# One part of a value table as dense tiles and a scattered weight matrix, the rest gathered, in a hybrid decoder layer

## The chip, the cores and the metric

The kernel runs on one core of a Trainium2 chip. The metric is the device time of one execution in microseconds (us), as a median of several runs; less is better.

## The reference, cut to what matters

The layer ends with a product-key (PEER) expert network over 256 tokens of width 2048, in two chunks c of 128 tokens. Each of 8 heads gives a token 16 experts out of 128 x 128 = 16384; an expert's number is 128 times its first key plus its second key, both from 0 to 127.

```
u = jnp.take(expert_u, ic, axis=0)                 # (c, k, d): 128 tokens x 128 experts x 2048
act = jax.nn.gelu(jnp.einsum('ckd,cd->ck', u, xc), approximate=False)
vv = jnp.take(expert_v, ic, axis=0)
return jnp.einsum('ck,ckd->cd', gc * act, vv)
```

A row of either table is 8 KB. What is added to the layer's state h is, for each token, the sum over its 128 experts of a weight (gate times activation) times the expert's value row. A final norm follows.

## The kernel before, in words

Everything ahead of the expert network (mixer, attention, cross-attention, the query projection `peer_wq`) is the same in both kernels. Work is ordered by hand: each engine has its own program, and they meet at semaphores.

The expert network is cut into GROUPS = 16 groups, one for each chunk c (2) and head (8). A group has TOP = 16 experts for each of the 128 tokens, which lie on the 128 partitions. For one k of a group, one indirect DMA gathers 128 rows of the table, one to each partition: 1 MB. So there are 256 gathers from the key table `peer_u` (u) and 256 from the value table `peer_v` (v). Both are issued by GpSimd (POOL).

- `u_ring` and `v_ring` have 4 slots of 1 MB each. In `period(p, q)` POOL issues, for k = 0 to 15 in turn, `gather_u` of group p (which waits until VectorE has done with the slot's last row, `dot_done`) and `gather_v` of group p - 1 (which waits for TensorE, `v_used`). POOL's program is in order: a gather behind one that waits has to wait as well.
- VectorE (DVE), in its own `period`, waits for the last values of the group before (`v_landed`), copies the indices for v, forms the weights (`weights`), finds the experts of the next group (`route`, a chain of some 30 short instructions) and their gates (`gates`), and then does 16 `dot_products` (L1079), one for each landed u slot.
- ScalarE (ACT) makes for each v gather a diagonal matrix of that k's weights (`diagonals`, L634); TensorE (PE) multiplies it with the v slot in four matmuls of 512 columns (L1493) and sums over all k in four PSUM banks, `misc` for chunk 0 and `acc` for chunk 1.
- In the last group 8 of the 16 value gathers (`BY_DVE`) are added by VectorE with a multiply-add over 2048 columns (L1167), the others by TensorE (L1501), so that both work on what lands last. `finish(0)` (the final norm of chunk 0) runs on VectorE between groups 13 and 15, `finish(1)` at the end.
- Loops over pairs of groups are hardware loops (`Fori`).

Of the kernel before, what the change touches and what calls it, by code (L numbers as in the profile page):

```python
# [33 lines left out]
def hybrid_layer(  # L34
# [8 lines left out]
    P = 128  # L43
# [13 lines left out]
    TOP = 16  # L57
# [84 lines left out]
    v_ring = put("v_ring", [P, 4, D], F32, at_split)  # L142
    final_gain = put("final_gain", [P, D], F32, at_raw)
# [23 lines left out]
    pT = put("pT", [P, 2, 3 * P], F32)  # L167
    xmax = put("xmax", [P, 2, TT], F32)
# [14 lines left out]
    picked = put("picked", [P, 2, TOP], F32)  # L183
# [6 lines left out]
    idx_u = put("idx_u", [P, 2, TOP], U32)  # L190
    idx_v = put("idx_v", [P, 2, TOP], U32)
    dots = put("dots", [P, 2, TOP], F32)
    acts = put("acts", [P, 2, TOP], F32)
    wts = put("wts", [P, 2, TOP], F32)
# [7 lines left out]
    with ExitStack() as ctx:  # L202
# [28 lines left out]
        v_landed = [sem(f"v_landed{s}") for s in range(4)]  # L231
        routed, idx_v_ready, nbest_ready, gexp_done = sem("routed"), sem("idx_v_ready"), sem("nbest_ready"), sem("gexp_done")
# [37 lines left out]
        BY_DVE = [2, 5, 8, 11, 12, 13, 14, 15]  # L270
        BY_PE = [k for k in range(TOP) if k not in BY_DVE]

        PC = CH * ITEMS["peer"][1]
        AHEAD = 12

# [7 lines left out]
        def _(sp):  # L286
# [71 lines left out]
        def _(pool):  # L358
# [23 lines left out]
            nc.gpsimd.memset(fones[:, :], 1.0).then_inc(consts, 1)  # L382
            nc.gpsimd.iota(iota[:, :], pattern=[[1, TOP]], base=0, channel_multiplier=0,
# [13 lines left out]
            def gather_u(p, q, k, fresh=False):  # L397
                if not (fresh and k < 4):

                    wait_apart(pool, dot_done, p * TOP + (k - 3))  # L400
                nc.gpsimd.indirect_dma_start(  # L401
                    out=u_ring[:, k % 4, :], out_offset=None, in_=u_rows,
                    in_offset=bass.IndirectOffsetOnAxis(ap=idx_u[:, q, k:k + 1], axis=0)).then_inc(u_landed[k % 4], 16)

            def gather_v(g, q, k, fresh=False):
                if not (fresh and k < 4):
# [6 lines left out]
            def period(p, q):  # L413
                pool.wait_ge(routed, p + 1)
                pool.wait_ge(idx_v_ready, p)
                for k in range(TOP):
                    gather_u(p, q, k)
                    gather_v(p - 1, 1 - q, k)

# [4 lines left out]
            for k in range(TOP):  # L424
                gather_u(0, 0, k, fresh=True)
            pool.wait_ge(routed, 2)
            for k in range(AHEAD):
                gather_u(1, 1, k)

            pool.wait_ge(idx_v_ready, 1)  # L430
            pool.wait_ge(peer_used, PC)
            for k in range(TOP):
                gather_v(0, 0, k, fresh=True)
                if k + AHEAD < TOP:
                    gather_u(1, 1, k + AHEAD)
            with pool.Fori(1, GROUPS // 2) as b:
                period(b * 2, 0)
                period(b * 2 + 1, 1)
            pool.wait_ge(idx_v_ready, GROUPS)
            for k in range(TOP):  # L440

                if k - 4 in BY_DVE:
# [1089 lines left out]
```

## Time and profile before

| what | value |
|---|---|
| median of 3 runs | 2108.12 us (2105.76 to 2112.22) |
| the profiled execution, its own time | 2111.71 us |
| span of its profile | 2109.9 us |
| its mean granted TensorE clock | 0.97 |
| TensorE, VectorE, ScalarE, GpSimd busy | 84%, 50%, 23%, 43% of the span |

The expert network takes the second part of the span, from about 750 us on. Shares of busy time are means over stages with different limits, so the stages are read one by one.

### The profile page before, as it was taken

To read this page: it belongs to the slowest core of one execution; us is meant where nothing else is said; L and a number is where in the kernel's file an instruction comes from. 1 tells how busy PE (TensorE), PEld (TensorE's weight loads), DVE (VectorE), ACT (ScalarE), POOL (GpSimd) and SP (SyncE) were. 2 spreads that over 40 slices of the span, in tenths; PEclk is the share of its full clock that TensorE was granted. 3 is DMA by queue.
4 is the path that set the end of the run, shared out by engine and by line. 5 is a ranking of instruction groups with operands and counts; after the bars stand their busy time and mean duration, and the time that the engine had idled before them with its cause. 6 is when DMAs were issued, how large, how long until landed. Compare 5 with 4: busy or idle time off the path is not lost.

```text
span 2109.9 us, 20817 instructions
## 1 busy us (share of the span) xinstructions
PE 1776.5 (84%) x7158; PEld 1134.4 (54%) x7161; DVE 1057.3 (50%) x1504; ACT 487.1 (23%) x802; POOL 911.5 (43%) x642
## 2 busy tenths in 40 slices
PE   7999999999999999797777777777777777758774
PEld 7998799888998898432332232322323223323232
DVE  4438343233333257534664664664664654655444
ACT  5345253345434411110110110111111111120111
POOL 4444143444432324444545545534535535535332
PEclk9999799999999999999999999999999999999998
DMA  8996154555535689999999999999999999999997
GB/s 204 235 194 158 67 182 160 195 187 189 167 120 194 195 331 391 364 368 422 414 415 423 416 422 421 420 420 421 416 419 421 417 422 415 420 421 382 422 414 274
DMA packets 150703, 682.56 MB, mean 324 GB/s; under 512 B 14632, under 2 KB 19824, under 8 KB 84336
## 3 DMA queue, kind: packets, MB, share of 16 engines
q0 software_dynamic: 73728, 536.90, 62.0%
q1 hardware_dynamic: 76912, 144.82, 23.1%
q8 instruction: 39, 0.64, 0.1%
q14 instruction: 24, 0.20, 0.0%
HBM read 679.58 MB, written 2.10 MB: 323 GB/s over the span
## 4 chain that ended last, share of the span: by engine, by line
PE 50%; DMA 34%; DVE 6%; issue 6%; POOL 2%; ACT 0%; DVEq 0%; SPq 0%; POOLq 0%; ACTq 0%
DMA v_ring<-in_peer_v_dram,idx_v 29%; PE acc L1493 6%; PE misc L1493 5%; PE acc L1202 5%; PE acc L1204 5%; PE acc L1203 5%; PE acc L1210 5%; PE acc L1209 5%; PE acc L1211 5%; PE acc L1471 4%; DMA u_ring<-in_peer_u_dram,idx_u 4%; PE acc L1432 1%; POOL u_ring L401 1%; DVE product L1079 1%; DMA raw<-in_w_in_dram 1%
## 5 line engine op out<-in xcount | busy, mean ns | idle before, releaser
L1079 DVE CUSTOM_DVE_ANT_0 product<-u_ring,hn 128x2048 bf16<-128x2048 f32 x256 | 586.7, 2292 | 497.3 <-DMA u_ring<-in_peer_u_dram,idx_u 491.4
L1493 PE MATMUL misc<-v_ring,diag 128*128 128x512 f32 x1024 | 480.3, 618 | 146.1 <-DMA v_ring<-in_peer_v_dram,idx_v 112.9
L1493 PE MATMUL acc<-v_ring,diag 128*128 128x512 f32 x896 | 423.9, 621 | 142.3 <-DMA v_ring<-in_peer_v_dram,idx_v 106.8
L409 POOL DMA_INDIRECT v_ring<-in_peer_v_dram,idx_v x240 | 283.6, 1182 | 436.4 <-PE misc L1493 216.6
L367 POOL TENSOR_TENSOR w_lo<-raw,w_hi 128x1024 fp32r<-128x1024 f32 x112 | 273.7, 2445 | 443.3 <-ACT w_hi L461 442.9
L401 POOL DMA_INDIRECT u_ring<-in_peer_u_dram,idx_u x256 | 325.7, 1272 | 263.7 <-DVE dots L1079 132.1
L1493 PEld LDWEIGHTS misc<-v_ring,diag 128*128 128x128 f32 x1024 | 192.2, 196 | 433.8 <-issue 259.4
L1493 PEld LDWEIGHTS acc<-v_ring,diag 128*128 128x128 f32 x896 | 168.7, 196 | 397.3 <-issue 230.8
L461 ACT ACTIVATE w_hi<-raw 128x1024 fp32r<-128x1024 f32 x224 | 236.8, 1059 | 337.6 <-PE acc L1211 151.3
L723 DVE TENSOR_TENSOR w_lo<-raw,w_hi 128x1024 fp32r<-128x1024 f32 x112 | 153.6, 1371 | 298.5 <-ACT w_hi L461 298.4
L634 ACT ACTIVATE diag<-ident,wts 128x128 f32<-128x128 f32 x240 | 91.4, 398 | 749.9 <-PE misc L1493 391.2
L1202 PE MATMUL acc<-t_hi,w_hi 128*128 128x256 f32 x896 | 255.7, 285 | 0.2 <-issue 0.2
L1203 PE MATMUL acc<-t_lo,w_hi 128*128 128x256 f32 x896 | 253.9, 283 | 0.0
L1204 PE MATMUL acc<-t_hi,w_lo 128*128 128x256 f32 x896 | 253.8, 283 | 0.0
L1209 PE MATMUL acc<-w_hi,t_hi 128*128 128x512 f32 x448 | 175.3, 391 | 0.0
L1211 PE MATMUL acc<-w_hi,t_lo 128*128 128x512 f32 x448 | 174.5, 389 | 0.0
L1210 PE MATMUL acc<-w_lo,t_hi 128*128 128x512 f32 x448 | 174.4, 389 | 0.0
L1202 PEld LDWEIGHTS acc<-t_hi,w_hi 128*128 128x128 f32 x896 | 172.3, 192 | 0.7 <-issue 0.4
L1203 PEld LDWEIGHTS acc<-t_lo,w_hi 128*128 128x128 f32 x896 | 172.3, 192 | 0.1
L1204 PEld LDWEIGHTS acc<-t_hi,w_lo 128*128 128x128 f32 x896 | 172.2, 192 | 0.0
L1211 PEld LDWEIGHTS acc<-w_hi,t_lo 128*128 128x128 f32 x448 | 84.1, 188 | 17.5
L1209 PEld LDWEIGHTS acc<-w_hi,t_hi 128*128 128x128 f32 x448 | 84.2, 188 | 17.3
(223 smaller groups left out, 1117.1 us busy)
## 6 DMA issues: line engine op xcount, KB each, us to landing
raw<-in_w_in_dram SPq DMA_DIRECT2D x64, 512.0 KB, 6.7
raw<-in_xattn_wk_dram SPq DMA_DIRECT2D x32, 512.0 KB, 4.2
raw<-in_xattn_wv_dram SPq DMA_DIRECT2D x32, 512.0 KB, 3.7
raw<-in_w_out_dram SPq DMA_DIRECT2D x32, 512.0 KB, 4.3
raw<-in_xattn_wq_dram SPq DMA_DIRECT2D x32, 512.0 KB, 4.2
raw<-in_xattn_wo_dram SPq DMA_DIRECT2D x32, 512.0 KB, 4.2
praw<-in_peer_wq_dram SPq DMA_DIRECT2D x32, 512.0 KB, 8.7
u_ring<-in_peer_u_dram,idx_u POOLq DMA_INDIRECT x256, 16.3
```

Of the source, the lines that this page charges most:

```text
L367: nc.gpsimd.tensor_tensor(w_lo[:, j % RING, :, :], raw[:, j % RING, :, :], w_hi[:, j % RING, :, :].bitcast(F32), ALU.subtract).then_inc(lo ...
L401: nc.gpsimd.indirect_dma_start(out=u_ring[:, k % 4, :], out_offset=None, in_=u_rows, in_offset=bass.IndirectOffsetOnAxis(ap=idx_u[:, q, k: ...
L409: nc.gpsimd.indirect_dma_start(out=v_ring[:, k % 4, :], out_offset=None, in_=v_rows, in_offset=bass.IndirectOffsetOnAxis(ap=idx_v[:, q, k: ...
L461: nc.scalar.activation(w_hi[:, j % RING, :, :], raw[:, j % RING, :, :], ACT.Copy).then_inc(hi_done, 1)
L1079: nc.vector.tensor_tensor_reduce(out=product[:, :], in0=u_ring[:, k % 4, :], in1=hn[:, c, :], scale=1.0, scalar=0.0, op0=ALU.mult, op1=ALU ...
L1202: nc.tensor.matmul(o, wh, hi[:, kt, :], start=first and ct % 2 == 0, stop=False, skip_group_check=True)
L1203: nc.tensor.matmul(o, wh, lo[:, kt, :], start=False, stop=False, skip_group_check=True)
L1204: ins = nc.tensor.matmul(o, wl, hi[:, kt, :], start=False, stop=last and ct % 2 == 1, skip_group_check=True)
L1209: nc.tensor.matmul(o, xh, w_hi[:, s, kk, :], start=first, stop=False)
L1210: nc.tensor.matmul(o, xh, w_lo[:, s, kk, :], start=False, stop=False)
L1211: ins = nc.tensor.matmul(o, xl, w_hi[:, s, kk, :], start=False, stop=last)
L1493: ins = nc.tensor.matmul(o, diag[:, k % 4, :], v_ring[:, k % 4, n * CW:(n + 1) * CW], start=False, stop=False)
```

## The change

Of the 128 first keys the last DENSE = 40 (88 to 127, FROM = 88) are no longer gathered. Their 40 x 128 value rows are loaded once, in order, as 40 tiles of 128 rows (1 MB each, `tile_landed`, from the SP queue, into the four slots of `u_ring` once the dot products are over). Each tile is multiplied by a 128 x 128 matrix of weights that has, for every second key and token, the token's weight of that expert: `wT0` and `wT1`, one for each chunk, [key, 40 tiles, token].

- These matrices are made in batches of WB = 8 tokens (32 batches in all). The lists of first keys, second keys and weights are transposed by TensorE (`turn_lists`) and copied by VectorE (`take_lists`); VectorE compares them with a row of key numbers (`one_hots`: one compare of 1024 columns, one compare and one multiply of 320 columns), TensorE multiplies the two one-hot matrices (`scatter_weights`, 8 matmuls of 40 columns) and ScalarE copies the result (`weights_T`). The 16 batches of chunk 0 stand between the dot products of groups 8 to 15, those of chunk 1 behind the last dot product.
- All 256 value gathers are still issued, but with a bound: `bounds_check` names the last row of first key 87, and `oob_is_err=False`. Their weight is set to zero where the first key is 88 or more (`low_wts`), so that whatever the slot holds there counts for nothing.
- Chunk 0's 128 value gathers go to TensorE through four slots, 8 in each of periods 2 to 7 and 10 in each of periods 8 to 15 (`v_share`), in POOL's order between the u gathers of that period. Before, each period had 16.
- Chunk 1's 128 value gathers are all issued behind the last dot product, into six slots (`V2S`), and VectorE adds them one by one with a multiply-add over 2048 columns (`add_values`); eight of them stand between the 16 last batches of `one_hots`. In that time TensorE multiplies the 40 tiles, each for both chunks (8 matmuls of 512 columns; for the last four tiles chunk 1's come after chunk 0's).
- `finish(0)` and `finish(1)` both stand at the end of VectorE's program, and the hardware loops are written out.

The core of the diff:

```
-            def gather_v(g, q, k, fresh=False):
-                if not (fresh and k < 4):
-                    wait_apart(pool, v_used, g * TOP + (k - 3))
+            def gather_v(n, slot, landed):
                 nc.gpsimd.indirect_dma_start(
-                    out=v_ring[:, k % 4, :], out_offset=None, in_=v_rows,
-                    in_offset=bass.IndirectOffsetOnAxis(ap=idx_v[:, q, k:k + 1], axis=0)).then_inc(v_landed[k % 4], 16)
+                    out=v_slot(slot), out_offset=None, in_=v_rows,
+                    in_offset=bass.IndirectOffsetOnAxis(ap=idx[:, n // TOP, n % TOP:n % TOP + 1], axis=0),
+                    bounds_check=FROM * KEYS - 1, oob_is_err=False).then_inc(landed, 16)
...
+            for p in range(1, GROUPS):
+                pool.wait_ge(routed, p + 1)
+                share = v_share(p)
+                for k in range(TOP):
+                    gather_u(p, k)
+                    for n in share[k * len(share) // TOP:(k + 1) * len(share) // TOP]:
+                        if n >= VS:
+                            pool.wait_ge(v_used, n - VS + 1)
+                        elif n == 2:
+                            pool.wait_ge(peer_used, PC - CH)
+                        gather_v(n, n % VS, v_landed[n % VS])
+            for m in range(TILE0):
+                if m >= V2S:
+                    pool.wait_ge(v_added, m - V2S + 1)
+                elif m < VS:
+                    pool.wait_ge(v_used, TILE0 - VS + m + 1)
...
+                gather_v(TILE0 + m, m % V2S, late_landed[m % V2S])
...
+            for t in range(DENSE):
+                if t < 4:
+                    sp.wait_ge(dot_done, GROUPS * TOP - 4 + t + 1)
+                else:
+                    sp.wait_ge(tile_used, t - 3)
+                sp.dma_start(u_ring[:, t % 4, :], v_rows[(FROM + t) * KEYS:(FROM + t + 1) * KEYS, :]).then_inc(tile_landed[t % 4], 16)
...
+            def period(g):
+                q, c = g % 2, g // PH
+                weights(g - 1)
+                if g + 1 < GROUPS:
...
+                    route(g + 1, 1 - q, (g + 1) // PH, (g + 1) % PH)
+                    gates(g + 1, 1 - q)
+                if g < PH:
+                    dot_products(g, q, c, range(0, TOP))
+                else:
+                    dot_products(g, q, c, range(0, 6))
+                    if g == PH:
+                        take_lists(0)
+                    one_hots(2 * (g - PH))
+                    dot_products(g, q, c, range(6, 12))
+                    one_hots(2 * (g - PH) + 1)
+                    dot_products(g, q, c, range(12, TOP))
...
+            def add_values(m):
+                dve.wait_ge(late_landed[m % V2S], 16 * (m // V2S + 1))
+                if m:
+                    dve.wait_ge(v_added, m)
+                nc.vector.scalar_tensor_tensor(y_sum[:, 1, :], v_slot(m % V2S), low_wts[:, PH + m // TOP, m % TOP:m % TOP + 1],
+                                               (y_sum if m else h)[:, 1, :], ALU.mult, ALU.add).then_inc(v_added, 1)
...
+            weights(GROUPS - 1)
+            take_lists(1)
+            for b in range(BATCHES):
+                one_hots(BATCHES + b)
+                if b % 2:
+                    add_values(b // 2)
+            for m in range(BATCHES // 2, TILE0):
+                add_values(m)
+            dve.wait_ge(v_added, TILE0)
             finish(0)
...
+            def one_hots(b):
+                t, q = b % BATCHES * WB, b % 2
+                if b >= 2:
+                    dve.wait_ge(wT_done, b - 1)
+                nc.vector.tensor_tensor(hotA[:, q, :, :], listsT[:, 1, t:t + WB].unsqueeze(2).to_broadcast([P, WB, KEYS]),
+                                        keys[:, :].unsqueeze(1).to_broadcast([P, WB, KEYS]), ALU.is_equal)
+                step(nc.vector.tensor_tensor(hotB[:, q, :, :], listsT[:, 0, t:t + WB].unsqueeze(2).to_broadcast([P, WB, DENSE]),
+                                             keys[:, FROM:].unsqueeze(1).to_broadcast([P, WB, DENSE]), ALU.is_equal))
+                nc.vector.tensor_tensor(hotB[:, q, :, :], hotB[:, q, :, :], listsT[:, 2, t:t + WB].unsqueeze(2).to_broadcast([P, WB, DENSE]),
+                                        ALU.mult).then_inc(hot_ready, 1)
...
+            def scatter_weights(b):
+                pe.wait_ge(hot_ready, b + 1)
...
+                for t in range(WB):
+                    ins = nc.tensor.matmul(acc[:, 0, b % 2, t * DENSE:(t + 1) * DENSE], hotA[:, b % 2, t, :], hotB[:, b % 2, t, :],
+                                           start=True, stop=True)
...
+            def dense_tile(t, c):
+                for i, o in enumerate((low, high)[c]):
+                    ins = nc.tensor.matmul(o, wT[c][:, t, :], u_ring[:, t % 4, i * CW:(i + 1) * CW], start=c == 1 and t == 0, stop=t == DENSE - 1)
...
+            for b in range(BATCHES, 2 * BATCHES):
+                scatter_weights(b)
+            pe.wait_ge(wT_copied, 2 * BATCHES)
+            for t in range(DENSE):
+                pe.wait_ge(tile_landed[t % 4], 16 * (t // 4 + 1))
+                ins = dense_tile(t, 0)
+                if t < DENSE - 4:
+                    dense_tile(t, 1).then_inc(tile_used, 1)
```

## Rows read from the trace of the kernel before

**Rows 1.** The page's table of slices: DMA share and GB/s, 52.7 us each.

```profile
DMA  8996154555535689999999999999999999999997
GB/s 204 235 194 158 67 182 160 195 187 189 167 120 194 195 331 391 364 368 422 414 415 423 416 422 421 420 420 421 416 419 421 417 422 415 420 421 382 422 414 274
```

**Rows 2.** Windows: us, busy time and count by engine, clock, DMA share, GB/s.

```profile
922.40:1962.90 1040.50, 784.46 (x1666) 312.65 (x1666) 594.15 (x899) 124.03 (x282) 511.02 (x416) 0.96 1.01 417
1482.40:1493.90 11.50, 7.78 (x19) 3.26 (x21) 9.03 (x40) 3.16 (x8) 2.73 (x3) 0.91 1.01 420
...
900.00:920.00 20.00, 20.00 (x48) 8.92 (x47) 0.00 (x0) 4.88 (x8) 6.58 (x7) 1.00 0.90 306
1520.00:1560.00 40.00, 29.84 (x66) 11.55 (x65) 18.40 (x16) 3.69 (x7) 16.70 (x17) 1.00 1.01 422
```

**Rows 3.** Groups by line, 780 to 2110 us: busy us, mean ns, idle before.

```profile
L1079 DVE CUSTOM_DVE_ANT_0 product<-u_ring,hn 128x2048 bf16<-128x2048 f32 x252 | 577.6, 2292 | 487.3 <-DMA u_ring<-in_peer_u_dram,idx_u 481.5 <-DVE gate L1060 2.7 <-DVE dots L1079 0.3
...
L401 POOL DMA_INDIRECT u_ring<-in_peer_u_dram,idx_u x248 | 317.9, 1282 | 218.8 <-DVE dots L1079 120.0 <-issue 72.5 <-PE misc L1493 17.1
...
L1167 DVE SCALAR_TENSOR_TENSOR y_sum<-v_ring,wts,y_sum 128x2048 f32<-128x2048 f32 x6 | 14.1, 2351 | 22.6 <-DMA v_ring<-in_peer_v_dram,idx_v 22.5
...
L1051 DVE TENSOR_TENSOR hot<-hot,top_at 128x512 f32<-128x512 f32 x15 | 10.4, 692 | 0.5
...
L1113 DVE TENSOR_TENSOR y_out<-y_sum,final_gain 128x1024 f32<-128x1024 f32 x2 | 2.5, 1226 | 0.2
```

**Rows 4.** VectorE's timeline, one period's seam (1478 to 1500 us).

```profile
1480.14 2.29 DVE L1079 CUSTOM_DVE_ANT_0 product<-u_ring,hn 128x2048 bf16<-128x2048 f32 x1 [2.67 <-DMA u_ring<-in_peer_u_dram,idx_u]
1482.36 0.08 DVE L1079 DVE_READ_ACCUMULATOR2_ANT dots<- 128x1 f32 x1
1482.69 0.17 DVE L1087 COPY idx_v<-idx_u 128x16 uint32<-128x16 uint32 x1 [0.25 <-DMA v_ring<-in_peer_v_dram,idx_v]
...
1493.85 2.29 DVE L1079 CUSTOM_DVE_ANT_0 product<-u_ring,hn 128x2048 bf16<-128x2048 f32 x1 [0.26 <-DVE gate L1060]
...
1496.19 2.29 DVE L1079 CUSTOM_DVE_ANT_0 product<-u_ring,hn 128x2048 bf16<-128x2048 f32 x1
```

**Rows 5.** GpSimd's timeline over the same seam.

```profile
1483.55 0.94 POOL L401 DMA_INDIRECT u_ring<-in_peer_u_dram,idx_u  x1 [0.30 <-issue]
1487.09 0.94 POOL L409 DMA_INDIRECT v_ring<-in_peer_v_dram,idx_v  x1 [2.60 <-PE misc L1493]
1496.96 2.33 POOL L401 DMA_INDIRECT u_ring<-in_peer_u_dram,idx_u  x1 [8.93 <-PE acc L1493]
```

**Rows 6.** The u gathers of 920 to 2045 us: issue to landing.

```profile
DMA to landing us min/median/max: 7.1/16.3/18.7
```

**Rows 7.** The last value gathers, 2050 to 2110 us: issue to landing.

```profile
DMA to landing us min/median/max: 5.5/8.2/9.9
```

**Rows 8.** The page's DMA queues: packets, MB, share of 16 engines.

```profile
q0 software_dynamic: 73728, 536.90, 62.0%
```

**Rows 9.** VectorE's timeline around the start of group 2.

```profile
859.65 2.29 DVE L1079 CUSTOM_DVE_ANT_0 product<-u_ring,hn 128x2048 bf16<-128x2048 f32 x1 [0.23 <-DMA u_ring<-in_peer_u_dram,idx_u]
...
872.07 2.29 DVE L1079 CUSTOM_DVE_ANT_0 product<-u_ring,hn 128x2048 bf16<-128x2048 f32 x1
...
884.52 2.29 DVE L1079 CUSTOM_DVE_ANT_0 product<-u_ring,hn 128x2048 bf16<-128x2048 f32 x1 [2.66 <-DMA u_ring<-in_peer_u_dram,idx_u]
```

**Rows 10.** TensorE's timeline, 900 to 920 us: values only.

```profile
899.66 20.76 PE L1493 MATMUL misc<-v_ring,diag 128*128 128x512 f32 x48
```

**Rows 11.** The chain that ended last, its last pieces: start, us, what.

```profile
2099.48 2.75 DVE y_sum L1108 x4
2102.28 0.04 issue
2102.32 1.24 DVE y_out L1113
...
2104.40 1.28 DVE y_out L1120
```

**Rows 12.** VectorE's timeline: the last dot product.

```profile
2048.02 2.29 DVE L1079 CUSTOM_DVE_ANT_0 product<-u_ring,hn 128x2048 bf16<-128x2048 f32 x1 [2.65 <-DMA u_ring<-in_peer_u_dram,idx_u]
```

More of the change, by code:

```diff
@@ L382, in _ @@
             nc.gpsimd.memset(fones[:, :], 1.0).then_inc(consts, 1)
+            nc.gpsimd.iota(keys[:, :], pattern=[[1, KEYS]], base=0, channel_multiplier=0,
+                           allow_small_or_imprecise_dtypes=True)
             nc.gpsimd.iota(iota[:, :], pattern=[[1, TOP]], base=0, channel_multiplier=0,
@@ L639, in gelu, with period @@
                 nc.scalar.activation(acts[:, q, :], dots[:, q, :], ACT.Gelu, scale=rstd[:, c:c + 1]).then_inc(gelu_done, 1)
-            def period(p, q, c, second=False, last=False):
-                if second:
-                    diagonals(p - 1, 1 - q, range(4), fresh=True)
-                if not last:
+            def period(p):
+                if p + 1 < GROUPS:
                     gate_exp(p + 1)
-                diagonals(p - 1, 1 - q, range(4 if second else 0, TOP))
-                gelu(p, q, c)
+                share = v_share(p)
+                diagonals(share[:4])
+                if p >= PH:
+                    weights_T(2 * (p - PH))
+                    diagonals(share[4:7])
+                    weights_T(2 * (p - PH) + 1)
+                    diagonals(share[7:])
+                else:
+                    diagonals(share[4:])
+                gelu(p, p % 2, p // PH)
             def finish(c):
@@ new lines, in _, with take_values, turn_lists @@
+            low = [misc[:, n, :] for n in range(4)]
+            high = [acc[:, n // 2, n % 2, :] for n in range(4)]
+            def take_values(n):
+                pe.wait_ge(v_landed[n % VS], 16 * (n // VS + 1))
+                pe.wait_ge(diag_ready, n + 1)
+                for i, o in enumerate(low):
+                    ins = nc.tensor.matmul(o, diag[:, n % 4, :], v_slot(n % VS)[:, i * CW:(i + 1) * CW], start=False, stop=False)
+                ins.then_inc(v_used, 1)
+            def turn_lists(c):
+                pe.wait_ge(wts_ready, (c + 1) * PH)
+                for a in range(3):
+                    ins = nc.tensor.transpose(acc[:, 1, 0, a * P:(a + 1) * P], lists[:, a, c, :], ident[:, :])
+                ins.then_inc(lists_done, 1)
@@ new lines, in _ @@
+            for o in low:
+                nc.tensor.matmul(o, zeros[:, 0:P], zeros[:, :], start=True, stop=False)
+            for p in range(2, GROUPS):
+                share = v_share(p)
+                if p == PH:
+                    turn_lists(0)
+                for n in share[:4]:
+                    take_values(n)
+                if p >= PH:
+                    scatter_weights(2 * (p - PH))
+                    for n in share[4:7]:
+                        take_values(n)
+                    scatter_weights(2 * (p - PH) + 1)
+                    for n in share[7:]:
+                        take_values(n)
+                else:
+                    for n in share[4:]:
+                        take_values(n)
@@ new lines, in _ @@
+            turn_lists(1)
+            for b in range(BATCHES, 2 * BATCHES):
+                scatter_weights(b)
[5 more added lines that the diff above has]
+                    dense_tile(t, 1).then_inc(tile_used, 1)
+            ins.then_inc(y_done, 1)
+            for t in range(DENSE - 4, DENSE):
+                ins = dense_tile(t, 1)
```

221 lines of the change are left out of this document (80 added, 141 removed).

## Prediction

> **What bounds the kernel now.** I read the page's slices first: in the expert network the DMA engines are full and move 414 to 423 GB/s in almost every slice [rows 1]. Windows confirm it for 13 whole periods: 1040.5 us at DMA share 1.01, while TensorE is busy for 75% and VectorE for 57% of it [rows 2]. The groups by line say who pays: VectorE is idle for 481.5 us in front of its dot products, waiting for u rows [rows 3]. So this stage moves bytes. One gather of 1.049 MB costs 1.049/0.422 = 2.48 us of the full DMA [rows 2]; a period of 32 gathers costs 80 us (1040.5/13). Fewer bytes should mean less time, as long as the engines stay full. Whether they do is the second question, and the timelines answer it. At a period's seam VectorE does no dot product from 1482.4 to 1493.85 us, 11.4 us of weights, routing and gates [rows 4]; no u slot comes free, and POOL issues nothing between 1488.0 and 1496.96 us [rows 5]. The DMA nevertheless stays at 1.01 [rows 2], because up to 8 MB are asked for at that moment (four u and four v slots): a gather takes 16.3 us from issue to landing where four per ring are out [rows 6], and 8 x 2.48 = 19.8 us of work covers the gap.
>
> **What the change removes and adds, in bytes.** I counted the experts that the reference chooses for its own inputs: 10006 of the 32768 have a first key of 88 or more (30.5%); 11414 rows of chunk 0 and 11348 of chunk 1 stay. If a row out of bounds costs nothing, a value gather shrinks to 0.695 x 2.48 = 1.72 us. 256 of them save 194 us of DMA, the 40 tiles cost 40 x 2.48 = 99 us. Net gain: 95 us, if the DMA is full throughout. What follows is how much of it is lost.
>
> **Start of period 2.** Before, 12 value gathers alone run ahead of period 2, at 306 GB/s [rows 2]; now none does. The dot products behind group 2's routing start at 872.07 us as before; with no v gathers beside them four take 4 x 2.34 = 9.3 us rather than lasting until 886.8 us [rows 9]. Period 2's seam starts at 881.4 us.
>
> **Periods 2 to 15.** Time zero is the end of the last dot product. The next one starts at 11.3 us (the copy of idx_v goes, a second small product of the weights comes) [rows 4]. Asked for at time zero are four u gathers and about two values, 4 x 2.48 + 2 x 1.72 = 13.4 us less what has already landed: the DMA is empty at about 11 us. The first slot is free at 11.3 + 2.34 = 13.6 us. The shortest time from issue to landing in the trace is 5.5 us [rows 7] and 7.1 us in the loaded stage [rows 6], each with others in front of it; for an empty DMA I take 5.2 us (POOL's 0.94, 2.48 of data, and the rest of the 5.5 as latency), so dot product 5's rows land at 18.8 us. The DMA has then stood still for some 5 us. From there 11 more u gathers land, each with half a value gather between: 2.48 + 0.86 = 3.34 us, so the last lands at 55.6 us and the period ends at 58.0 us. With 10 values, 3.55 us each: 60.2 us. VectorE's own work is less (11.3 + 16 x 2.34 = 48.7 us, and 53.4 us with two batches of one_hots), so the batches hide under the waits for u. They would cost 4.7 us a period if the cover were gone.
>
> A page of the Trainium skill (DMA: Bandwidth & Descriptors, section Anatomy of one DMA, the SWDGE path) fits one gather as 2.0 us plus bytes at 436 GB/s, 4.4 us for one of these. By it each gap would be 0.8 us shorter and my sum 10 us less. No row here shows a gather alone on an empty queue.
>
 So periods 2 to 7 take 6 x 60.1 = 361 us, 8 to 14 take 7 x 62.9 = 440 us, and 15, which has no routing, 26 gathers' worth: 16 x 2.48 + 10 x 1.72 + 2.6 = 59.5 us. Together 860 us against 16 x 4.96 us and more each before.
>
> By the Trainium skill (same page, section The descriptor swizzle) engine and partition are tied in a fixed pattern, four neighbours and the four 32 further on; counted that way the figures are 21 and 23% for six gathers and 5 to 6% for 128. A page that speaks against this change; by even dealing the sum would be some 47 us less.
>
> **Behind the last dot product.** Time zero again. Weights, transposes and take_lists: about 5 us. A batch of one_hots is one compare of 1024 columns, like L1113's 1.23 us, and two of 320, between nothing and L1051's 0.69 us for 512; by the slope of these two (1.04 ns a column) 0.49 us each: 2.3 us with its step, 16 of them 37 us. Eight additions at 2.39 us (2.35 and a semaphore) [rows 3]: 19 us. VectorE is through with the batches at 61 us, and only then can TensorE start the tiles. Its cost: 48 matmul records in 20.76 us, 0.43 us each, 8 for one slot and chunk [rows 10]: 3.43 us, 6.9 us a tile, 275 us in all, to 336 us. VectorE's 120 other additions take 287 us, to 348 us at least. The DMA has, from 61 us until the last tile is in at 309 us, 36 tiles (89 us) and 159 us for value gathers of 1.72 us, or 1.84 us with the 7% of the busiest engine over a long window (a ring of six evens out less than all 128, a busiest engine that changes costs a new ring): 86. With 14 landed before, 28 are left at 309 us; then VectorE's pace of 2.39 us rules: 67 us. The last addition ends at about 380 us. Bounds: 350 us (VectorE alone), 404 us (22% for uneven rows). Tail: finish takes 6.2 us, from 2099.5 to 2105.7 [rows 11], now twice and none of it hidden, then 4.2 us to the span's end as before: 16.8 us. Before, all that stood behind the last dot product (over at 2050.3 us [rows 12]) took 59.6 us; now 397.
>
> **Sum.** 881.4 + 860 + 380 + 16.8 = 2138 us of span, 2140 with the 1.8 us that lie around it, against 2111.7 for the profiled execution before: 1.3% more. Scaled to the median of 2108.1 that is about 2137 us. The 95 us are outweighed by 13 seams x 5 us = 65, uneven rows 47, an idle DMA in the first 61 us (27 us of the 61), VectorE's pace at the end (19) and finish (0) in the open (6), less some 35 us that the start gains; the rest is rounding between the two ways of adding.
>
> **Rivals.**
> - *Full DMA at the seams (faster).* If more is asked for at a seam than I count, or a landed gather comes sooner, the gap goes: 6 x 53.6 + 8 x 57 = 777 us for the periods and, with even rows, 364 us behind them: 2040 us. For it: the seam before shows no gap [rows 2]. Against: half the values stand in POOL's order. It decides from 2.4 us a seam down: 13 x 2.6 = 34 us saved brings the time to 0.3% under before.
> - *Gaps, but even rows.* 2138 - 31 - 16 = 2091 us, 0.8% faster. For it: nothing in a row; against it the 8 rows an engine.
> - *Rows out of bounds are still moved.* Then a value gather stays at 2.48 us: periods 6 x 62.1 + 7 x 65.5 + 64.5 = 896 us, behind them 64 gathers by 309 us and 50 left at 2.48 us, 436 us: 2230 us, 5.8% more. No row here shows a bounded gather.
> - *Dearer than counted.* POOL's bounded gather above 2.4 us (1.28 us now [rows 3]), one_hots without cover (8 x 4.7 = 38 us), or batches of chunk 1 that take twice 37 us: 2170 to 2200 us.
>
> **Chances.** Forecast, 2110 to 2170 us: 0.46. Even rows, 2075 to 2110: 0.17. Full DMA, 2030 to 2075: 0.17. Rows still moved: 0.08. Dearer, 2170 to 2200: 0.12. 0.3% (6 us) is about what a measurement can tell from no change. Faster (below 2102): 0.36; within: 0.10; slower: 0.54. The range 2050 to 2190 us leaves about half of the full-DMA case and all of the rows-still-moved case outside; the forecast's own range is 2110 to 2170.
>
> **What the profile after would show.** q0 with about 186 MB of values beside 268 MB of u (455 MB); DMA share below 0.95 in periods, with a dip behind each seam; seams 58 to 63 us apart, DVE idle in front of L1079's successor on DMA about 0.8 us each; the last dot product near 1742 us; dense matmuls for 275 us and ending 40 us ahead of the last addition. The prediction is wrong if periods are under 56 us (no gap), if q0 still moves 537 MB, or if the stretch behind the last dot product is far from 397 us.

## The result and the profile after

The changed kernel takes 2211.1 us (2210.8 to 2211.8, 4 runs) against 2109.8 us: 1.048 times as long, 95% interval 1.046 to 1.050. I had forecast 1.3% more, 2137 us, and a range up to 2190. The profiled execution's span is 2209.0 us, 71 us more than my sum of 2138: the direction was right, the size was not.

The page's slices (granted clock, DMA share, GB/s), 55 us each, and q0's line (packets, MB, share of 16 engines):

```profile
PEclk9999899999999998777888888888989976999985
DMA  8995255665545798888888988888988975999986
GB/s 205 235 189 154 77 182 169 191 186 186 159 147 180 263 402 339 355 348 355 339 348 362 403 355 348 345 347 351 401 354 351 407 305 182 397 412 392 394 316 211
...
q0 software_dynamic: 73728, 454.97, 52.2%
```

q0 moves 455 MB in place of 537 [rows 8], as counted: rows out of bounds move no bytes, though their packets are still counted. But where the DMA was full at 420 GB/s [rows 1], it now runs at some 350. Windows of periods 3 to 7, of the stretch with the tiles, and of the end (busy time and count by engine, clock, DMA share, GB/s), against [rows 2]:

```profile
940.98:1260.99 320.01, 189.07 (x321) 73.46 (x320) 228.21 (x346) 30.25 (x66) 218.32 (x121) 0.81 0.89 357
1900.00:2000.00 100.00, 100.00 (x235) 44.27 (x234) 77.56 (x33) 0.00 (x0) 66.40 (x34) 1.00 1.01 405
2110.00:2180.00 70.00, 24.84 (x58) 10.64 (x56) 65.06 (x28) 0.00 (x0) 53.58 (x27) 0.71 0.85 292
```

The five numbers behind the length are the engines'. GpSimd (the fifth) is busy for 218 of 320 us. In 1040 us before it was 511, for 416 gathers, 1.23 us each; now it is 1.80 us each, 218.32/121. The groups of 878 to 1792 us show the same, against [rows 3]:

```profile
L1116 DVE CUSTOM_DVE_ANT_0 product<-u_ring,hn 128x2048 bf16<-128x2048 f32 x225 | 515.9, 2293 | 224.1 <-DMA u_ring<-in_peer_u_dram,idx 216.8 <-DVE dots L1116 0.5
L430 POOL DMA_INDIRECT u_ring<-in_peer_u_dram,idx x222 | 432.0, 1946 | 226.1 <-DVE dots L1116 166.4 <-issue 56.7 <-PE misc L1512 3.0
...
L436 POOL DMA_INDIRECT v_low<-in_peer_v_dram,idx x66 | 106.6, 1615 | 25.7 <-issue 20.1 <-PE misc L1512 5.6
L436 POOL DMA_INDIRECT v_high<-in_peer_v_dram,idx x65 | 102.1, 1571 | 22.1 <-issue 19.5 <-PE misc L1512 2.6
```

VectorE still waits for u rows, 217 us, but their transfer was asked for late: L430 costs 1.95 us in place of 1.28. In these 914 us GpSimd waited for TensorE for 3.0 us in front of u gathers and 8.2 us in front of value gathers, less than 1 us a period. So values used late, at the lower granted clock (0.81 in periods 3 to 7, 0.96 before), are not the cause.

The two timelines beside one another tell why. GpSimd behind the seam of period 3, then VectorE over the same time:

```profile
941.72 0.95 POOL L430 DMA_INDIRECT u_ring<-in_peer_u_dram,idx  x1 [0.30 <-issue]
942.97 1.01 POOL L436 DMA_INDIRECT v_low<-in_peer_v_dram,idx  x1 [0.30 <-issue]
954.06 2.99 POOL L430 DMA_INDIRECT u_ring<-in_peer_u_dram,idx  x1 [10.08 <-DVE dots L1116]
957.36 2.14 POOL L430 DMA_INDIRECT u_ring<-in_peer_u_dram,idx  x1 [0.30 <-issue]
959.80 2.20 POOL L436 DMA_INDIRECT v_high<-in_peer_v_dram,idx  x1 [0.30 <-issue]
...
967.81 1.01 POOL L436 DMA_INDIRECT v_high<-in_peer_v_dram,idx  x1 [0.30 <-issue]
969.12 0.95 POOL L430 DMA_INDIRECT u_ring<-in_peer_u_dram,idx  x1 [0.30 <-issue]
```

```profile
953.94 2.29 DVE L1116 CUSTOM_DVE_ANT_0 product<-u_ring,hn 128x2048 bf16<-128x2048 f32 x1
...
956.39 2.29 DVE L1116 CUSTOM_DVE_ANT_0 product<-u_ring,hn 128x2048 bf16<-128x2048 f32 x1
...
958.83 2.29 DVE L1116 CUSTOM_DVE_ANT_0 product<-u_ring,hn 128x2048 bf16<-128x2048 f32 x1
```

The gather of 957.36 ends at 959.50, 0.82 us behind the end of the dot product of 956.39 (958.68). The next ends at 962.00, 0.88 us behind the next dot product. Gathers of 0.95 and 1.01 us stand where VectorE does no dot product. A gather instruction that meets a dot product waits for its end. This is the *port theory* of the experiments: GpSimd reads the 128 indices from SBUF through something it shares with VectorE's second SBUF input. The Trainium skill (SBUF — State Buffer, section Who interferes with whom) has the rule: a VectorE instruction with two SBUF inputs contends with a GpSimd instruction that reads SBUF. The rows above agree with it: 2.14 and 2.20 us beside dot products, whose two inputs lie in SBUF, and 0.95 and 1.01 us without one. The rival is the *uneven-rows theory*, that my sum was right in kind and only the busiest DMA engine or a transfer's latency was priced too low.

The end of the program, VectorE's timeline, against [rows 11]: the last addition ends at 2192.9 us, both finishes and the output take 16.1 us more.

```profile
2188.11 4.80 DVE L1144 SCALAR_TENSOR_TENSOR y_sum<-v_low,low_wts,y_sum 128x2048 f32<-128x2048 f32 x2
...
2198.81 2.48 DVE L1155 TENSOR_TENSOR y_sum<-acc,y_sum 128x512 f32<-128x512 f32 x4
...
2203.47 1.28 DVE L1166 SCALAR_TENSOR_TENSOR y_out<-y_sum,rstd,final_gain 128x1024 f32<-128x1024 f32 x1
```

### The profile page after: what moved, and what is told of

Its sections match the earlier page's. It is cut to its first block, busy times and chain, and to the rows that moved or that the text cites. A ratio compares the mean times of both kernels' runs of the same rounds, so it can differ in the third digit from the quotient of the medians.

```text
span 2209.0 us, 20330 instructions
## 1 busy us (share of the span) xinstructions
PE 1778.7 (81%) x7347; PEld 1193.0 (54%) x7347; DVE 1399.7 (63%) x1722; ACT 446.8 (20%) x713; POOL 1231.4 (56%) x643
## 4 chain that ended last, share of the span: by engine, by line
PE 35%; POOL 23%; DMA 15%; issue 14%; DVE 12%; ACT 0%; SPq 0%; DVEq 0%; POOLq 0%; ACTq 0%
POOL u_ring L430 15%; DMA u_ring<-in_peer_u_dram,idx 6%; PE acc L1223 5%; PE acc L1225 5%; PE acc L1224 5%; PE acc L1231 4%; PE acc L1230 4%; PE acc L1232 4%; DVE y_sum L1144 4%; POOL v_high L436 4%; DMA v_low<-in_peer_v_dram,idx 4%; POOL v_low L436 4%; DMA v_more<-in_peer_v_dram,idx 3%; DVE product L1116 2%; PE acc L1526 2%
## 5 line engine op out<-in xcount | busy, mean ns | idle before, releaser
L430 POOL DMA_INDIRECT u_ring<-in_peer_u_dram,idx x256 | 488.4, 1908 | 320.4 <-DVE dots L1116 223.3
L1512 PE MATMUL misc<-v_high,diag 128*128 128x512 f32 x512 | 289.4, 720 | 173.2 <-DMA v_high<-in_peer_v_dram,idx 150.3
L1512 PE MATMUL misc<-v_low,diag 128*128 128x512 f32 x512 | 290.5, 723 | 160.2 <-DMA v_low<-in_peer_v_dram,idx 80.3
L1512 PEld LDWEIGHTS misc<-v_high,diag 128*128 128x128 f32 x512 | 112.3, 229 | 343.8 <-DMA v_high<-in_peer_v_dram,idx 191.4
L1512 PEld LDWEIGHTS misc<-v_low,diag 128*128 128x128 f32 x512 | 113.7, 231 | 329.7 <-issue 219.8
L436 POOL DMA_INDIRECT v_low<-in_peer_v_dram,idx x108 | 193.1, 1788 | 79.0 <-DVE y_sum L1144 44.5
L436 POOL DMA_INDIRECT v_high<-in_peer_v_dram,idx x106 | 184.8, 1744 | 67.4 <-issue 29.2
L1532 PE MATMUL misc<-u_ring,wT 128*128 128x512 f32 x320 | 145.9, 601 | 0.5 <-ACT wT L655 0.5
L1532 PE MATMUL acc<-u_ring,wT 128*128 128x512 f32 x320 | 143.4, 592 | 0.0
```

Source lines behind the costliest of these rows:

```text
L430: nc.gpsimd.indirect_dma_start(out=u_ring[:, k % 4, :], out_offset=None, in_=u_rows, in_offset=bass.IndirectOffsetOnAxis(ap=idx[:, p, k:k ...
L436: nc.gpsimd.indirect_dma_start(out=v_slot(slot), out_offset=None, in_=v_rows, in_offset=bass.IndirectOffsetOnAxis(ap=idx[:, n // TOP, n % ...
L1512: ins = nc.tensor.matmul(o, diag[:, n % 4, :], v_slot(n % VS)[:, i * CW:(i + 1) * CW], start=False, stop=False)
L1532: ins = nc.tensor.matmul(o, wT[c][:, t, :], u_ring[:, t % 4, i * CW:(i + 1) * CW], start=c == 1 and t == 0, stop=t == DENSE - 1)
```

## The experiments

A period below is the distance between two runs of `weights` in VectorE's timeline (L1089: 878.49, 940.98, ... 1260.99, ... 1793.21 us in the changed kernel). "Periods 2 to 7" and "8 to 15" are means of 6 and 8 such distances. Ratios are to the kernel before.

### The operation by itself

The core of a kernel of its own; idx holds the five patterns of indices, `a` and `b` lie in SBUF, `ps` in PSUM:

```
for kind in range(5):
    for g in range(4):
        pool.wait_ge(landed, 16 * count[0])
        for k in range(6):
            gather(kind, 6 * g + k)
...
if s == 0:    tensor_tensor_reduce(out=prod, in0=a, in1=b, ...)
elif s == 1:  tensor_tensor_reduce(out=prod, in0=a, in1=ps, ...)
elif s == 2:  scalar_tensor_tensor(sumf, a, dots[:, 0:1], sumf, ALU.mult, ALU.add)
elif s == 3:  scalar_tensor_tensor(ps, a, dots[:, 0:1], ps, ALU.mult, ALU.add)
else:         tensor_tensor(sumf, a, b, ALU.mult)
```

> A kernel that computes nothing of the layer: 128-row gathers of 1 MB from the value table, in batches of six that are drained in between, with all rows in bounds, with 30.5% out of bounds by chance, with every fourth partition out of bounds, with the lower 32 partitions out of bounds, and with all out of bounds; four gathers alone before that; then 12 gathers with all rows out of bounds each beside a continuous stream of VectorE operations of 2048 columns: product with sum of two SBUF inputs, the same with one input in PSUM, multiply-add of SBUF with SBUF, multiply-add of SBUF with PSUM, plain product of two SBUF inputs. Port theory: GpSimd's instruction takes 0.95 to 1.1 us beside the operations with one SBUF input and 2 us or more beside those with two. Uneven-rows theory: with the lower 32 partitions out of bounds a batch takes as long as with all rows (14.9 us and latency), with every fourth out of bounds 25% less, by chance 10 to 15% less. If the rest is dealt out evenly: 25% less in both, 30% by chance. A lone gather lands 5.2 us after its issue by the prediction.

GpSimd's timeline: one gather from inside each of the five streams of VectorE operations, in that order.

```profile
392.08 2.03 POOL L123 DMA_INDIRECT ring<-in_peer_v_dram,idx  x1 [0.30 <-issue]
...
423.52 0.99 POOL L123 DMA_INDIRECT ring<-in_peer_v_dram,idx  x1 [0.30 <-issue]
...
457.71 2.08 POOL L123 DMA_INDIRECT ring<-in_peer_v_dram,idx  x1 [0.30 <-issue]
...
489.83 0.99 POOL L123 DMA_INDIRECT ring<-in_peer_v_dram,idx  x1 [0.30 <-issue]
...
524.82 2.02 POOL L123 DMA_INDIRECT ring<-in_peer_v_dram,idx  x1 [0.30 <-issue]
```

With two inputs in SBUF a gather instruction takes 2.02 to 2.08 us, with one of them in PSUM 0.99 us, as with VectorE idle. VectorE's time is the same in both (2.29 and 2.29 us, 2.35 and 2.36). GpSimd then goes in step with VectorE, one gather in 2.33 us (2.39 us beside the multiply-add). So the port theory holds for the instruction alone, with no value row moved.

The distance between the starts of batches of six, a mean of four, from GpSimd's timeline:

| indices out of bounds | us a batch | starts |
|---|---|---|
| none | 20.3 | 56.31 to 137.67 |
| 30.5% by chance | 16.9 | 137.67 to 205.19 |
| every fourth partition | 16.8 | 205.19 to 272.38 |
| the lower 32 partitions | 19.2 | 272.38 to 349.14 |
| all | 10.1 | 349.14 to 389.42 |

A quarter of the rows gone from every fourth partition saves 3.5 us of 14.9 us of data, as by bytes (3.7); the same number gone from one block of partitions saves 1.1 us. So an engine's rows do depend on the partition. The sizes that I had expected for this theory were missed twice: the block should have saved nothing, and the reason for its 1.1 us stays open; rows gone by chance save 3.5 us, 23% of the data and not 10 to 15%, where bytes alone give 4.5. The last row holds one pause of GpSimd of 3 us; its other batches take 9.4 to 9.5 us. A lone gather has landed 6.1 to 6.5 us after the start of its instruction, where I took 5.2. The profile's own count from issue to landing, 5.3 to 5.7 us here, starts some 0.8 us later, and I had read the 5.5 us of [rows 7] as if it held POOL's 0.94. The 4.4 us that the prediction worked out by the Trainium skill (DMA: Bandwidth & Descriptors, section Anatomy of one DMA, the SWDGE path) is further off still; the measurement decides.

```profile
37.60 0.99 POOL L123 DMA_INDIRECT ring<-in_peer_v_dram,idx  x1 [5.40 <-DMA ring<-in_peer_v_dram,idx]
43.76 0.99 POOL L123 DMA_INDIRECT ring<-in_peer_v_dram,idx  x1 [5.16 <-DMA ring<-in_peer_v_dram,idx]
49.81 0.99 POOL L123 DMA_INDIRECT ring<-in_peer_v_dram,idx  x1 [5.06 <-DMA ring<-in_peer_v_dram,idx]
```

### The second input moved to PSUM, in the kernel

```
+            def hn_of(g, c):
+                return acc[:, :, :, :].rearrange("p a b n -> p (a b n)") if 2 <= g < PH else hn[:, c, :]
...
-  tensor_tensor_reduce(out=product[:, :], in0=u_ring[:, k % 4, :], in1=hn[:, c, :], ...)
+  tensor_tensor_reduce(out=product[:, :], in0=u_ring[:, k % 4, :], in1=hn_of(g, c), ...)
...
+                if g == 2:
+                    dve.wait_ge(scores_ready, items)
+                    step(nc.vector.tensor_copy(acc[:, :, :, :].rearrange("p a b n -> p (a b n)"), hn[:, 0, :]))
```

> The changed kernel, but in periods 2 to 7 the dot products read the normed state of chunk 0 from PSUM (the four acc banks, idle then; one copy more at the start of period 2) instead of SBUF, so VectorE has one SBUF input in place of two. Port theory (a gather instruction on GpSimd must read its indices from SBUF and waits as long as VectorE runs an operation with two SBUF inputs, so 24 to 26 gathers a period at 1.82 us plus 0.30 us and 10 us idle make the period): gathers in periods 2 to 7 fall from a mean of 1.82 us to about 1.05 us, those periods from about 63.8 us to 58 to 60 us, periods 8 to 15 stay at 66.6 us, the whole is 20 to 30 us faster than the changed kernel. Uneven-rows theory (a slot is full only when the busiest DMA engine is through): the six periods stay within 1 us. TensorE-clock theory (values are late because TensorE is at 1.2 GHz for part of the time): nothing changes either.

GpSimd's groups from 941 to 1200 us, in this kernel:

```profile
L430 POOL DMA_INDIRECT u_ring<-in_peer_u_dram,idx x68 | 64.3, 945 | 152.2 <-DVE dots L1119 147.9 <-issue 4.4
L436 POOL DMA_INDIRECT v_low<-in_peer_v_dram,idx x17 | 17.1, 1009 | 5.2 <-issue 5.2
```

The u gather falls to 0.945 us; the periods 2 to 7 go from 63.75 to 60.6 us, the periods 8 to 15, where nothing was changed, stay (66.53 and 66.49). The time is 1.044 (1.042 to 1.046), 2199 us: 12 us less by the medians, 17 by the spans of the profiled executions, 9 by the ratios, less than the 20 to 30 I had expected, and the periods are just above my 58 to 60. One of the six carries much of the gain: period 5 takes 67.3 us in the changed kernel and 60.1 here, the other five fall from 63.0 to 60.7 on the mean. The experiment decides for the port theory, as both others let these periods stand, and the granted clock of periods 3 to 7 is 0.82, as it was. It also leaves my own sum standing: I had forecast 60.1 us for these periods.

### No value rows, alone and with PSUM

```
-                    bounds_check=FROM * KEYS - 1, oob_is_err=False).then_inc(landed, 16)
+                    bounds_check=0, oob_is_err=False).then_inc(landed, 16)
```

> The changed kernel with the bound of the value gathers at row 0, so that practically no value row is moved; the values of first keys 0 to 87 are left out of the result. All instructions and waits stay. Port theory: the periods hardly shorten, to 60 to 63 us from 63.8 and to 63 to 65 us from 66.6, because GpSimd's instruction stream makes them, not bytes; behind the last dot product the additions go at GpSimd's and VectorE's common pace of 2.46 us from the first to the last. Uneven-rows theory: with nothing to be uneven the period is VectorE's 48.7 us plus at most 3 us, and 53.4 us with the one-hot batches; the whole is 130 us or more faster.

> Both at once: the dot products of periods 2 to 7 read the normed state from PSUM, and the value gathers move practically no rows (the values of first keys 0 to 87 are left out). Each alone left these periods at about 60 us (60.6 and 60.1 on the mean, 63.8 before). Port theory with uneven rows behind it: the two are covers for one another; with GpSimd free (0.97 us a gather) and no value bytes the periods fall to VectorE's own 48.7 us and little more, 49 to 52 us. If only the port counted: not below 58 us. If only rows counted: as with no rows alone, 60 us.

| periods 2 to 7, us | hn in SBUF | hn in PSUM |
|---|---|---|
| 70% of the value rows | 63.75 | 60.6 |
| no value rows | 60.2 | 51.4 |

| periods 8 to 15 (hn in SBUF in all) | | |
|---|---|---|
| 70% of the value rows | 66.5 | 66.5 |
| no value rows | 63.1 | 63.1 |

All value bytes gone save 3.6 us, the port freed saves 3.1 us, both save 12.3. The two bounds lie close together and hide one another: with the port held, 24 gathers at about 2.1 us (instruction and 0.3 us) and a seam of 10 us make 60 us whatever is moved; with it free, the rows make 60. For periods 8 to 15 only the rows were taken away. The whole is 1.006 (1.004 to 1.008) without rows and 0.981 (0.980 to 0.983) with both; the values of first keys 0 to 87 are left out of both times. Behind the last dot product, without rows, GpSimd's gathers take 2.15 us from the first to the last and the additions come every 2.45 us:

```profile
L436 POOL DMA_INDIRECT v_low<-in_peer_v_dram,idx x39 | 84.8, 2174 | 16.7 <-issue 11.6 <-DVE y_sum L1144 5.1
```

### All value rows

```
-                    bounds_check=FROM * KEYS - 1, oob_is_err=False).then_inc(landed, 16)
+                    bounds_check=KEYS * KEYS - 1, oob_is_err=False).then_inc(landed, 16)
```

> The changed kernel with the bound at the table's end, so that every value row is moved although 30% of them get weight zero. Port theory: the added bytes (0.76 us a gather) show little in the periods, 64 to 67 us for 63.8 and 67 to 70 for 66.6, as the DMA is not full there; behind the last dot product, where it is full while the tiles come, 128 x 0.76 = 97 us would be added at most, 60 to 90 us by my guess. Uneven-rows theory: full gathers are even, so the 2.1 and 2.6 us that I put on unevenness go as the bytes come: 62.1 and 65.5 us, no change or a little less than now.

1.091 (1.090 to 1.093), 2298 us. Periods 2 to 7 take 64.7 us, 1 us more for 6 us of bytes; 8 to 15 take 70.5 us, 4 more for 7.6 us of bytes (I had expected 67 to 70); the stretch from the last weights to the last addition grows from 400 to 446 us, less than I had guessed. What leaving rows out saved in this kernel is thus 87 us, by the medians, of the 194 by bytes.

### The seam

```
-                    route(g + 1, 1 - q, (g + 1) // PH, (g + 1) % PH)
-                    gates(g + 1, 1 - q)
...
+                route_part(0)
+                dot_products(g, q, c, range(0, 3))
+                route_part(1)
+                dot_products(g, q, c, range(3, 6))
+                route_part(2)
+                dot_products(g, q, c, range(6, 8))
+                if g + 1 < GROUPS:
+                    gates(g + 1, 1 - q)
...
-                if p + 1 < GROUPS:
-                    gate_exp(p + 1)
                 share = v_share(p)
-                diagonals(share[:4])
+                diagonals(share[:2])
+                if p + 1 < GROUPS:
+                    gate_exp(p + 1)
+                diagonals(share[2:4])
```

> The changed kernel with the routing of the next group cut in three parts: before dot product 0, behind dot product 2 and behind dot product 5, the gates behind dot product 7, the one-hot batches behind 8 and 12; ScalarE's exponential moves behind two diagonals. VectorE does the same work. Both theories say that the seam costs: GpSimd idle for 10 us and the DMA empty for about 5 us in each of 13 seams. Port theory: without the seam GpSimd's 24 x 2.12 = 51 us are no longer the bound; the DMA's 53.6 to 57 us or VectorE's 48.7 to 53.4 us are, periods of 54 to 59 us, the whole 90 to 120 us faster. Uneven-rows theory as I put it in the prediction: periods shorter by the 5 us of the empty DMA alone, 65 us in all.

> Routing in three parts and, in periods 2 to 7, the normed state in PSUM. Port theory: the periods 2 to 7, 58.5 us with the split alone, fall to the DMA's 53.6 us plus what uneven rows cost, 54 to 57 us; periods 8 to 15 stay at 61.4 us; the whole 10 to 25 us faster than the split alone, 2117 to 2132 us, still above the kernel before. Uneven-rows theory: periods 2 to 7 stay within 1 us of 58.5.

Split alone: 1.017 (1.015 to 1.019), 2142 us; periods 58.5 and 61.4 us, 5.3 and 5.1 less than in the changed kernel. The whole gains 69 us, not the 90 to 120 that I expected once I had the port in mind. With PSUM as well: 1.013 (1.011 to 1.015), 2133 us, where I had expected 2117 to 2132, and periods 2 to 7 at 56.3 us. So the split is worth 5.3 us a period while the port is held and 4.3 us once it is free (60.6 to 56.3). Windows of periods 3 to 7, first of PSUM alone, then of both:

```profile
941.38:1242.79 301.41, 187.08 (x321) 72.74 (x320) 227.80 (x346) 30.34 (x66) 115.97 (x121) 0.82 0.93 380
```

```profile
935.70:1216.70 281.00, 186.24 (x321) 72.12 (x320) 227.11 (x346) 29.74 (x66) 118.19 (x121) 0.85 1.00 410
```

With both the DMA is at 1.00 again and the period 2.7 us above the 53.6 us of its bytes. The share alone doesn't say that the DMA is the bound: with the split alone it is already 0.99 in these periods, at 390 GB/s, and freeing the port still saves 2.1 us a period.

The gap at the seam can be seen directly. DMA share behind the seam of period 3, half a microsecond a digit: the changed kernel from 941 us, with PSUM from 941 us, with the split from 935 us.

```profile
DMA  9999999999998999987753100000000009379999
```

```profile
DMA  9999999999999999977674220000009878999999
```

```profile
DMA  9999999999989999999987899899989999969979
```

It is 0 for 5.0, 3.0 and 0 us. Over the seams of periods 3 to 7 the means are 4.7, 2.4 and 0 us, and 0 in the kernel before. So about 2.3 us of the idle DMA at such a seam are the port's as well: the first gather takes 2.99 us there (954.06 above) and 0.95 us with the port free. Even this best version of the changed kernel stays 1.3% behind the kernel before.

### Uneven rows, in the kernel before

The kernel before with the bound alone, and then with fixed partitions out of bounds in its value gathers:

```
                     in_offset=bass.IndirectOffsetOnAxis(ap=idx_v[:, q, k:k + 1], axis=0),
+                    bounds_check=88 * KEYS - 1, oob_is_err=False).then_inc(v_landed[k % 4], 16)
```

```
+            step(nc.vector.tensor_scalar(pand[:, :], pnum[:, :], 3, None, ALU.bitwise_and))
+            step(nc.vector.tensor_scalar(away[:, :], pand[:, :], 3.0, 100000.0, ALU.is_equal, ALU.mult))
...
-                nc.vector.tensor_copy(idx_v[:, q, :], idx_u[:, q, :]).then_inc(idx_v_ready, 1)
+                nc.vector.tensor_scalar(idx_v[:, q, :], idx_u[:, q, :], away[:, 0:1], None, ALU.add).then_inc(idx_v_ready, 1)
```

(for the lower 32 partitions: mask 96, compared with 0; the bound is the table's end in both).

> The kernel before with nothing but the bound on its value gathers (first keys 88 to 127 are not moved; their weights stay, so whatever the slot holds is added in place of these values). Four u and four v slots in flight, 16 gathers of each a period. By bytes the period falls from 80.0 to 16 x 2.48 + 16 x 1.72 = 67.2 us, with uneven rows 71 to 72 us. Port theory: 32 gathers at 1.5 to 1.8 us plus 0.3 us are 58 to 67 us and 8 to 10 us idle at the seam, so GpSimd is about as much of a bound as the DMA: 69 to 74 us. The whole 100 to 160 us faster than before.

> The kernel before with a bound on its value gathers and indices changed so that every fourth partition is out of bounds in all of them (these tokens' values are left out). 96 of 128 rows are left, 8 MB in flight, 16 u and 16 v gathers a period. By bytes the period is 16 x 2.48 + 16 x 1.86 = 69.4 us. The bound at first key 88 moved fewer bytes (67.2 us by bytes) and took 75.7 us. Uneven-rows theory: these left-out rows are even (each DMA engine loses two of eight), so the period is 69.5 to 71.5 us, shorter than with fewer but uneven rows. Port theory alone: as many gathers, as long a wait for VectorE, 75 to 77 us again.

> The same with the lower 32 partitions out of bounds: the same bytes as in the run with every fourth, 69.4 us a period if bytes or instructions count. Uneven-rows theory: half of the DMA engines lose nothing, so the period stays at 79 to 80 us, as in the kernel before, and the whole within 1% of it.

| value rows left | by bytes | periods 2 to 7 | ratio |
|---|---|---|---|
| all | 79.4 | 80.2 | 1 |
| first keys 0 to 87, 70% | 67.2 | 75.7 | 0.966 (0.964 to 0.968) |
| every fourth partition out, 75% | 69.4 | 74.3 | 0.958 (0.956 to 0.959) |
| lower 32 partitions out, 75% | 69.4 | 80.0 | 1.000 (0.999 to 1.001) |

Windows from 922 to 1700 us, every fourth partition, then the lower 32:

```profile
922.00:1700.00 778.00, 632.81 (x1349) 254.32 (x1348) 479.67 (x721) 96.57 (x222) 578.29 (x336) 0.96 0.98 394
```

```profile
922.00:1700.00 778.00, 588.99 (x1259) 235.49 (x1258) 445.86 (x679) 88.92 (x205) 392.48 (x313) 0.97 0.93 368
```

The same bytes, 5.8 us a period apart: which partitions lose rows decides, and with a block of them gone nothing is gained at all. That settles the tie of engine and partition. But with even rows the period is not the 69.5 to 71.5 us that this theory gave either; GpSimd's 336 gathers take 1.72 us each there (1.23 in the kernel before over the same time), and 1.72 + 0.3 for each of 32 and some 10 us at the seam are 75 us. So GpSimd is likely to be the bound there, as fewer bytes let VectorE come round faster and its dot products meet more of the gathers. That is argued, not shown: the port wasn't freed in this kernel, and the DMA share reads 0.98. With 70% of the rows the period is 75.7 us where I had said 69 to 74, and the whole is 71 us faster, not 100 to 160.

### Uneven rows, in the changed kernel

PSUM as above, and a second table of indices (`idx_w`, the index plus 100000 in every fourth partition) for the value gathers.

> The changed kernel with the normed state of chunk 0 in PSUM for periods 2 to 7 and every fourth partition out of bounds in place of first keys from 88 on (values are left out and others doubled). A value gather is 1.86 us of DMA in place of 1.72, but even. With uneven rows and free GpSimd the periods 2 to 7 took 60.6 us. Uneven-rows theory: 58.0 us by my sum for even rows, and 8 x 0.14 = 1.1 us for the bytes, so 59 us or a little less: 1 to 2 us shorter with more bytes. If unevenness cost nothing there: 61 to 62 us.

Periods 2 to 7: 60.0 us against 60.6, with 1.1 us more of bytes. By that unevenness costs 1.7 us a period there, where I had counted 2.1; less than the "59 us or a little less" I expected, and the difference of 0.6 us rests on six periods each. 1.038 (1.037 to 1.040).

## Why the prediction was wrong, point by point

- **Bytes.** Right: 455 MB in q0, nothing moved for rows out of bounds.
- **Start of period 2.** 881.4 us forecast, 878.1 measured.
- **The seam.** Right in kind: the DMA runs empty, for 4.7 us on the mean where I had some 5. That the size agrees is partly luck. I had counted a gather instruction of 0.94 us; it takes 2.99, which makes about 2.3 us of the gap, and with the port free the gap is 2.4 us. A lone gather's 6.1 us in place of 5.2 would have made it longer.
- **Periods 2 to 15: the step that failed.** Forecast 860 us, measured 914.7, 55 of the 71 us. I let the DMA's pace and VectorE's own work make the period and put GpSimd's gathers among the rivals, as a bound only "above 2.4 us", from a mean of 1.28 us. That was wrong twice. The mean is no property of the instruction: it was low because VectorE, waiting for u rows for 481.5 us of some 1330 [rows 3], seldom stood in its way. And 2.4 us is no threshold: with 10 us idle at the seam, 24 gathers of 1.8 us plus 0.3 already fill 60 us. The row was there: the u gather behind the seam took 2.33 us while VectorE ran dot products back to back [rows 4, 5], and I read only its start. With the port freed the periods 2 to 7 take 60.6 us where I said 60.1; so of the 3.65 us that they were too long, 3.15 are the port. For periods 8 to 15 (66.5 for 62.9) the same excess is put down to it by likeness alone: four free PSUM banks for chunk 1's state aren't there, so it wasn't tried.
- **Uneven rows.** Right in kind: engines are tied to partitions. In size 1.7 us a period against 2.1, by one comparison of six periods each.
- **Behind the last dot product.** 380 us forecast, 400 measured. One-hot batches as forecast (61 us). Without rows the stretch is 355 us against my 348 for VectorE alone, as VectorE and GpSimd go in step at 2.45 us, not 2.39; the rows add 45 us where I had 32 (my terms give 376 us; 4 of the 380 have no term). The tiles' matmuls took 277 us, as forecast (275). The miss is in the value gathers beside the tiles: 309 us behind the last dot product I had 28 additions left, the trace has 36 (the line below: window, busy time and count of L1144, clock, DMA share, GB/s), and 8 of 2.45 us are the 20 us. From 1900 to 2100 us the DMA moved 398 GB/s at a share of 1.00; with all value rows it moved 421 at 1.01. That fits uneven rows, priced too low here, but no run separates it.

```profile
2101.80:2209.00 107.20, 83.75 (x36) 0.67 0.74 260
```

- **Tail.** 16.8 us forecast (its terms add up to 16.6), 16.1 measured.
- **The rivals.** "Full DMA at the seams" did not come; the split shows what it would have brought, 4.3 to 5.3 us each. "Rows still moved" is excluded by q0; made to happen it costs 87 us. "Dearer than counted" named the right instruction, with a wrong price, a range that ended at 2200 and 0.12 of chance.

So why is the change slower than no change, by 101 us, when its bytes promise 95 us less? At the seams, because half as many value gathers cover them: splitting the routing brings back 69 us. At the port: freeing it in periods 2 to 7 brings back 9 to 17 us, but 9 once the routing is split; the two overlap, so they must not be added, and for periods 8 to 15 the port is not shown. And behind the last dot product: that stretch ends in additions that come at 2.45 us from one engine, while the DMA is at 0.85 and less.

## What to carry to other kernels

Taking load off the resource that bounds a kernel also takes away the waits that kept other engines apart; read the mean time of an instruction together with what its neighbours do in that time, and price it by the occurrences in which a neighbour is at work beside it, not by its mean, when the change will bring the neighbours closer. A gather queue in program order needs enough in flight to cover the longest stretch in which its slots aren't freed: count that in bytes before halving the number of gathers in it. And rows left out of a gather save time only as far as they are spread evenly over the DMA engines, which here means over the groups of partitions.

## What the runs showed of the hardware

- GpSimd's indirect gather of 128 rows: 0.95 to 1.0 us alone, 2.02 to 2.08 us beside VectorE operations of 2048 columns with both inputs in SBUF, 0.99 us when one of them is in PSUM; it ends 0.8 us behind the VectorE operation that it meets. VectorE loses nothing.
- Up to eight gathers of 1 MB asked for kept the DMA at 1.01 through a stretch of 11.4 us in which no slot came free; with four of 1 MB and about two of 0.7 MB it stood still for 4.0 to 6.0 us at each of five seams.
- Indices out of bounds move no bytes (455 MB in place of 537, with as many packets); a gather with all 128 of them out of bounds still costs its 0.99 us of instruction.
- A quarter of the rows left out in one block of 32 partitions saves nothing of the kernel's time (ratio 1.000, 0.999 to 1.001), in every fourth partition 4.2%. The Trainium skill's fixed pattern (DMA: Bandwidth & Descriptors, section The descriptor swizzle) agrees: every fourth partition takes two rows from each engine, the lower 32 take four from half of them.
